# NSA stage of a 13-stage fp32 kernel: gates computed transposed, values unit one place earlier, position additions between two evictions

## The reference, cut to what matters

```python
q, k_c, v_c, k_s, v_s, k_w, v_w, gates = split(h @ w_in)        # 1024 + 6*256 + 48 columns
gates = sigmoid(gates).reshape(B, S, 3, G, R)                   # 48 per token
def compress(kv, pos, w1, w2):                                  # 15 blocks of 32 tokens
    blk = kv[:, cmp_idx] + pos                                  # position additions
    return gelu(blk @ w1) @ w2                                  # (60, 2048) @ (2048, 256) @ (256, 64)
kc, vc = compress(k_c, ...), compress(v_c, ...)
o_cmp = softmax(q @ kc.T, mask) @ vc
o = gates[0] * o_cmp + gates[1] * o_slc + gates[2] * o_win      # o_slc, o_win: causal attention
return o @ w_out
```

## Time and profile before

| | us |
|---|---|
| median of 3 runs | 2328.58 (2327.27 to 2328.65) |
| the profiled execution | 2329.75 |
| its span | 2327.9 |
| mean granted clock | 0.983 |
| PE, DVE, ACT busy | 2261.5, 1780.5, 1159.4 |

### The profile page before, as it was taken

How to read it: one execution, slowest core, us unless ns; L and a number is a source line. 1 busy time by engine, 2 the same in 40 slices (tenths; PEclk the granted TensorE clock), 3 DMA queues, 4 the chain that set the end, 5 groups by cost and what they waited for, 6 DMA issues and landing times.

```text
span 2327.9 us, 37353 instructions
## 1 busy us (share of the span) xinstructions
PE 2261.5 (97%) x14904; PEld 2012.6 (86%) x14904; DVE 1780.5 (76%) x3490; ACT 1159.4 (50%) x2082; POOL 0.2 (0%) x4
## 2 busy tenths in 40 slices
PE   7999999999999999999999999999999999998998
PEld 7968889898889988897988887788888889978997
DVE  7588987779887798777798865577877876478877
ACT  4486554565553555447655634534222235375333
POOL 0000000000000000000000000000000000000000
PEclk9799999999999999989999999999999999999999
DMA  6315666446565565641565532023554522423653
GB/s 239 116 43 206 239 197 215 152 163 233 199 212 186 191 239 192 223 170 38 182 234 198 183 115 85 1 73 120 171 189 154 165 89 100 136 83 133 236 202 118
DMA packets 70155, 373.52 MB, mean 160 GB/s; under 512 B 7392, under 2 KB 16736, under 8 KB 37984
## 3 DMA queue, kind: packets, MB, share of 16 engines
q1 hardware_dynamic: 61472, 361.52, 45.5%
q10 hardware_dynamic: 8512, 9.63, 1.4%
HBM read 369.03 MB, written 1.05 MB: 159 GB/s over the span
## 4 chain that ended last, share of the span: by engine, by line
PE 84%; DVE 9%; ACT 3%; DMA 3%; issue 1%; ACTq 0%; DVEq 0%
PE ps L470 79%; DVE w_lo L1682 3%; DMA w_raw<-weights 2%; PE ps L793 2%; DVE hid_f L2051 1%; PE ps L776 1%; DVE hid_f L2071 1%; ACT w_hi L1128 1%; PE ps L731 1%; PE ps L721 1%; DVE a_both L1682 0%; DVE X L1934 0%; DVE X L1808 0%; ACT p_ring L1260 0%; DMA sm<-small 0%
## 5 line engine op out<-in xcount | busy, mean ns | idle before, releaser
L470 PE MATMUL ps<-a_both,w_hi 128*128 128x256 f32 (+1 forms) x4960 | 1209.4, 330 | 27.6 <-DVE a_both L1739 10.6
L470 PEld LDWEIGHTS ps<-a_both,w_hi 128*128 128x128 f32 x4960 | 828.7, 192 | 105.3 <-issue 29.0
L470 PE MATMUL ps<-a_both,w_lo 128*128 128x256 f32 (+1 forms) x3184 | 902.1, 292 | 0.0
L1682 DVE TENSOR_TENSOR w_lo<-w_raw,w_hi 128x1024 fp32r<-128x1024 f32 (+1 forms) x632 | 707.9, 1148 | 88.4 <-ACT w_hi L1128 81.8
L470 PEld LDWEIGHTS ps<-a_both,w_lo 128*128 128x128 f32 x3184 | 608.2, 191 | 26.3
L1128 ACT CAST w_hi<-w_raw 128x1024 fp32r<-128x1024 f32 (+2 forms) x452 | 418.5, 975 | 417.1 <-DMA w_raw<-weights 416.3
L470 PE MATMUL ps<-hid_both,w_hi 128*128 128x512 f32 (+1 forms) x2088 | 578.3, 355 | 8.4 <-DVE hid_both L1682 5.6
L470 PEld LDWEIGHTS ps<-hid_both,w_hi 128*128 128x128 f32 x2088 | 367.1, 190 | 65.8 <-DVE hid_both L1682 4.4
L470 PE MATMUL ps<-hid_both,w_lo 128*128 128x256 f32 (+1 forms) x1396 | 421.1, 305 | 0.0
L470 PEld LDWEIGHTS ps<-hid_both,w_lo 128*128 128x128 f32 x1396 | 265.2, 190 | 14.4
L1134 ACT CAST w_hi<-w_raw 128x1024 fp32r<-128x1024 f32 (+2 forms) x180 | 183.6, 1020 | 0.6 <-DMA w_raw<-weights 0.6
(11 more groups left out here) (215 smaller groups left out, 1957.1 us busy)
## 6 DMA issues: line engine op xcount, KB each, us to landing
w_raw<-weights SPq DMA_DIRECT2D x250, 1024.0 KB, 4.8
pe_sb<-weights SPq DMA_DIRECT2D x96, 512.0 KB, 5.6
w_raw<-weights SPq DMA_DIRECT2D x64, 704.0 KB, 4.0
pe_sb<-na_bias ACTq DMA_DIRECT2D x32, 128.0 KB, 2.2
X<-x_t SPq DMA_DIRECT2D x2, 512.0 KB, 7.1
X<-c_rows ACTq DMA_DIRECT2D x2, 512.0 KB, 4.1
qk<-qk ACTq DMA_DIRECT2D x4, 256.0 KB, 7.0
qk<-ctx_t ACTq DMA_DIRECT2D x1, 1024.0 KB, 5.7
```

Of the source, the lines that this page charges most:

```text
L470: return nc.tensor.matmul(out, stationary, moving, start=start, stop=stop)
L1682: return v.tensor_tensor(out, a, b.bitcast(F32), ALU.subtract)
```

## The change

It does three things. (1) The gates are made transposed: the 48 gate columns of the weights are stationary, the 256 tokens moving, 24 matmuls in place of 48. ScalarE copies the 48x256 result from PSUM to `t_ring`, TensorE transposes it back in two pieces into bank 5, and ScalarE's sigmoid reads that and signals `gates`, for which TensorE waits ahead of turn 1's scores. The gelu transposes now stand ahead of the gates. (2) The stage's units have another order: 0, 1; queries 2 to 4; 5 compress(0,0); 6 query; 7 compress(0,1); 8 keys; 9 compress(1,0); 10 keys; 11 compress(1,1); 12 values; 13 small; the rest as it was. (3) VectorE makes the position additions between the two evictions of units 1 to 4, and the `w_lo` work of unit 14 stands behind the gelu copies.

On TensorE:

```diff
-                for _ in range(4):
+                for _ in range(3):
                     fm_unit("AA", a)
...
-                compress(0, 0)
-                fm_unit("AA", a)
-                compress(0, 1)
-                fm_unit("AA", a)
-                compress(1, 0)
+                for kv in range(2):
+                    for h in range(2):
+                        compress(kv, h)
+                        if (kv, h) != (1, 1):
+                            fm_unit("AA", a)
                 values_unit()
-                compress(1, 1)
-                u, [(gb, gp, (g_ready, _)), (kb, kp, (k_ready, _)), (vb, vp, (v_ready, _))] = start_unit("AAD")
-                start_product("A", gp)
-                for tt in range(2):
-                    c0 = 2 * P + 2 * HD
-                    last = tm(ps[:, gb, tt * 3 * HEADS:(tt + 1) * 3 * HEADS], u % SLOTS,
-                              lambda k: slice(c0 + k * 3 * HEADS, c0 + (k + 1) * 3 * HEADS),
-                              raw_tokens(tt))
-                last.then_inc(g_ready, 1)
                 pe.wait_ge(nsa[j]["gelu"], 2)
...
                 last.then_inc(nsa[j]["gelu_t"], 1)
+                u, [(gb, gp, (g_ready, _)), (kb, kp, (k_ready, _)), (vb, vp, (v_ready, _))] = start_unit("AAD")
+                start_product("A", gp)
+                c0 = 2 * P + 2 * HD
+                for k, (xh, xl) in enumerate(a):
+                    c = slice(c0 + k * 3 * HEADS, c0 + (k + 1) * 3 * HEADS)
+                    weights_at(c)
+                    out = ps[0:3 * HEADS, gb, 0:S]
+                    mm(out, w_hi[:, u % SLOTS, c], xh, k == 0, False)
+                    mm(out, w_hi[:, u % SLOTS, c], xl, False, False)
+                    last = mm(out, w_lo[:, u % SLOTS, c], xh, False, k == KD - 1)
+                last.then_inc(g_ready, 1)
                 pe.wait_ge(nsa[j]["gelu_ready"], 2)
...
                 last.then_inc(v_ready, 1)
+                pe.wait_ge(nsa[j]["gates_copied"], 1)
+                for tt in range(2):
+                    last = nc.tensor.transpose(ps[:, GATE_BANK, tt * 3 * HEADS:(tt + 1) * 3 * HEADS], gates_t[:, tt * P:(tt + 1) * P],
+                                               ident[0:3 * HEADS, 0:3 * HEADS])
+                last.then_inc(nsa[j]["gates_t"], 1)
...
                         pe.wait_ge(nsa[j]["cmp_shifted"], 1)
+                        pe.wait_ge(nsa[j]["gates"], 1)
```

On ScalarE:

```diff
-                for tt in range(2):
-                    ins = nc.scalar.activation(gate[:, tt, :], ps[:, bank, tt * 3 * HEADS:(tt + 1) * 3 * HEADS], ACT.Sigmoid,
-                                               scale=stat[:, tt:tt + 1])
-                ins.then_inc(taken["A"], 1)
+                nc.scalar.copy(gates_t, ps[0:3 * HEADS, bank, 0:S]).then_inc(s["gates_copied"], 1)
...
-                ins.then_inc(taken["A"], 1)
+                ins.then_inc(taken["A"], 2)
+                act.wait_ge(s["gates_t"], 1)
+                for tt in range(2):
+                    ins = nc.scalar.activation(gate[:, tt, :], ps[:, GATE_BANK, tt * 3 * HEADS:(tt + 1) * 3 * HEADS], ACT.Sigmoid,
+                                               scale=stat[:, tt:tt + 1])
+                ins.then_inc(s["gates"], 1)
                 ahead(u)
```

On VectorE:

```diff
+                def unit_around(dst, between):
+                    u, made = next_unit("AA")
+                    scaled(made[0], dst(0))
+                    between(u)
+                    scaled(made[1], dst(1))
+                    ahead(u)
...
+                ahead(scaled_unit(compressed(0)))
                 sync()
-                dve.wait_ge(taken["A"], cnt.n["A"])
-                add_positions(0, False)
-                query(1)
-                dve.wait_ge(s["shifted"], 32)
-                add_positions(0, True)
-                query(2)
+                unit_around(compressed(1), lambda u: first_positions(0))
+                unit_around(queries(0), lambda u: first_positions(1))
+                unit_around(queries(1), lambda u: moved_positions(0))
                 blocks_low(0)
-                add_positions(1, False)
-                query(3)
-                add_positions(1, True)
+                unit_around(queries(2), lambda u: moved_positions(1))
+                skip("")
+                ahead(scaled_unit(queries(3)))
                 step(v.memset(vg_hi.bitcast(F32), 0.0))
                 skip("")
+                blocks_low(1)
                 ahead(keys(0))
-                blocks_low(1)
...
-                values("DD", 0, KV)
-                skip("")
+                values_unit, made = next_unit("DD")
+                evict_values(range(2), made, 0, KV)
...
                 ins.then_inc(s["gelu_ready"], 1)
+                ahead(values_unit)
                 ahead(u)
```

More of the change, by code:

```diff
@@ L223, in program @@
                for n in ("nsa0", "nsa1", "moba0", "mla0", "na0")}
-        nsa = [{e: sem(f"{e}{j}") for e in ("shifted", "blocks", "blocks_hi", "blocks_ready", "gelu", "gelu_t", "gelu_ready", "cmp_scores",
+        nsa = [{e: sem(f"{e}{j}") for e in ("shifted", "blocks", "blocks_hi", "blocks_ready", "gelu", "gelu_t", "gelu_ready", "gates_copied",
+                                            "gates_t", "gates", "cmp_scores",
                                             "cmp_shifted", "cmp_exp", "cmp_p", "cmp_t", "cmp_t_taken")}
@@ L398, in program @@
         GEL_BANK = 4
+        GATE_BANK = 5
+        gates_t = t_ring[0:3 * HEADS, 0, 0:S]
         c_act = [X[:, KD // 2 * j:KD // 2 * (j + 1), CTX] for j in range(2)]
@@ L1390, in run_nsa @@
                 skip("")
+                skip("AA")
+                u, _ = next_unit("")
+                gelu(1, u)
+                ahead(u)
                 skip("DD")
-                skip("")
-                gelu(1, cnt.n["unit"] - 1)
                 u, made = next_unit("AAD")
@@ L2142, in run_nsa @@
                 norm_row()
-                for kv in range(2):
-                    ahead(scaled_unit(lambda pair: k_sb[:, 4 + kv, pair * S:(pair + 1) * S]))
                 v_rep = [h.rearrange("p (m g r c) -> p m g r c", m=2, g=GROUPS, r=REP) for h in (vg_hi, vg_lo)]
@@ L2165, in add_positions @@
                     ins.then_inc(s["blocks"], 1)
-                def query(i):
-                    ahead(scaled_unit(lambda m: q_sb[:, 2 * i + m, 0:S]))
                 def keys(br):
@@ L2176, in blocks_low, with compressed, first_positions, moved_positions @@
                     minus(blk_lo[:, c], blk_f[:, c], blk_hi[:, c]).then_inc(s["blocks_ready"], 1)
-                query(0)
-                sync()
-                dve.wait_ge(taken["A"], cnt.n["A"])
-                add_positions(0, False)
-                query(1)
-                dve.wait_ge(s["shifted"], 32)
-                add_positions(0, True)
-                query(2)
+                def compressed(kv):
+                    return lambda pair: k_sb[:, 4 + kv, pair * S:(pair + 1) * S]
+                def unit_around(dst, between):
[3 more added lines that the diff above has]
+                    scaled(made[1], dst(1))
+                    ahead(u)
+                def first_positions(kv):
+                    dve.wait_ge(taken["A"], 2 * kv + 2 + before)
+                    add_positions(kv, False)
+                def moved_positions(kv):
+                    dve.wait_ge(s["shifted"], 32)
+                    add_positions(kv, True)
+                def queries(i):
+                    return lambda m: q_sb[:, 2 * i + m, 0:S]
+                before = cnt.n["A"]
+                ahead(scaled_unit(compressed(0)))
+                sync()
+                unit_around(compressed(1), lambda u: first_positions(0))
+                unit_around(queries(0), lambda u: first_positions(1))
+                unit_around(queries(1), lambda u: moved_positions(0))
                 blocks_low(0)
-                add_positions(1, False)
-                query(3)
-                add_positions(1, True)
+                unit_around(queries(2), lambda u: moved_positions(1))
+                skip("")
+                ahead(scaled_unit(queries(3)))
                 step(v.memset(vg_hi.bitcast(F32), 0.0))
                 skip("")
+                blocks_low(1)
                 ahead(keys(0))
-                blocks_low(1)
                 step(v.memset(vg_lo.bitcast(F32), 0.0))
```

12 lines of the change are left out of this document (6 added, 6 removed).

## The result

The changed kernel takes 2309.07 us (median of 4 runs, 2307.88 to 2310.39), the kernel before 2328.57 (4 runs, 2327.27 to 2328.65). The ratio is 0.9916, with a 95% interval of 0.9905 to 0.9927: 19.5 us faster. The forecast was 2305.5 in a range of 2299 to 2315. The profiled execution took 2308.13 us. The title has the values unit one place earlier. By the order of the units it stands one place later (12, it was 11), behind the last compress unit.

A forecast was written before the change was run, and what follows sets the result against it. TensorE, busy 2261.5 of 2327.9 us, was taken to bound the kernel. Stage gains of 14.1 and 11.0 us, less 2 for the clock, gave 23.1: 2306.65 profiled, 1.17 above the median, so 2305.5, range 2299 to 2315.

The forecast's parts named there:

- Up to the small unit: Units 1 to 12: eviction wait of 0.86 us gone, waits of 0.9 and 0.3 added, values end at 79.4.
- Gates: Small unit at full clock: 24 gate matmuls in 2.73 us, against 8.1 before; v product ends at 85.9.
- The chain through VectorE: Sigmoid, cast and w_lo of unit 15, value copies, mask, p_cmp: its transposes start at 97.35, TensorE waiting some 3 us.
- The clock term: Short fall to half clock from the v product through the compressed scores: 1 us per stage, between 0 and 3.5.
- the 77.15 us without it: Forecast length of each NSA stage, unit 1 to first p_cmp transpose, before the clock's price; 91.27 and 88.17 before.
- the slack of some 3 us before L902: TensorE's forecast wait for p_cmp before its first transpose, some 3 us, said to take up a late clock fall.
- 1 (no fall): Clock doesn't fall between the v product and turn 1: gain 25.1 us, time 2303.5; chance 0.22.
- 2 (low until turn 1): Clock falls with the v product, down until turn 1: gains 7.6 and 4.5 us, time 2316.5; chance 0.12.
- 3 (low for the turns): Clock falls at waits before p_cmp's transposes, down for 16 turns: costs 44 us in both stages, 2349; chance 0.02.
- 4 (VectorE late): Compress run: VectorE doesn't keep up, units 6 and 9 wait 4 us more per stage, 2313.5; chance 0.09.
- The number: Whole kernel: 23.1 us less, from 2329.75 to 2306.65 for a profiled execution, 2305.5 for the median.
- the likeliest case: Whole kernel, forecast with a short clock fall: 2305.5 us, range 2302 to 2309; chance 0.52.

The follow-up runs named there:

- kernels 6: Changed kernel with blocks_low(1) ahead of unit 9's w_lo work and the w_lo copies of unit 15 moved behind p_cmp; 2306.95 us.
- kernel 7: Changed kernel with the 24 matmuls of v in each NSA stage moving 256 columns where 64 are used; 2307.66 us.
- kernel 8: Changed kernel with the four gelu transposes put back behind the gates' matmuls; 2319.16 us.
- 10: Changed kernel with blocks_low(1) ahead of unit 9's w_lo work and v's matmuls moving 256 columns; 2305.47 us.
- kernel 1: Kernel before with only the gates formed transposed, unit order and position additions as they were; 2325.22 us, ratio 0.9988.
- 2: Changed kernel with the old gate matmuls of 48 moving columns, new unit order kept; 2326.8 us, ratio 0.9994.
- 3: Changed kernel with the position additions back behind both evictions and the w_lo work of the unit two ahead; 2312.7 us.
- kernel 5: Kernel before with its 48 gate matmuls widened from 48 to 256 moving columns, the extra ones unused; 2325.03 us.
- 9: Changed kernel with the old 48 gate matmuls, widened from 48 to 256 moving columns; 2316.23 us.
- 12: Kernel 10 with unit 15's w_lo copies behind p_cmp, ScalarE's table loaded early and compressed-score matmuls moving 128 columns; 2300.32 us.

## Why the prediction was right, step by step

- **Up to the small unit**: right. The wait before unit 4 is gone, compress(1,0) waits 1.12 us (forecast 0.9), unit 6 waits 0.79 (0.3, within its bounds; in kernels 6, 7, 8 and 10 it is 0.28 to 0.42). The values unit ends at 79.6 (79.4).
- **Gates**: right, 82.91 - 80.12 = 2.79 us for 24 (2.73), at full clock, and no wait before them or before the k product. v ends at 86.3 (85.9).
- **The chain through VectorE**: right as to its members and its end, 97.73 us (97.3). That TensorE would wait for it some 3 us was wrong for this kernel: the clock had used up that slack. Kernels 7 and 10, where the clock stayed up, show the wait at 1.16 to 2.31 us.
- **The clock term**: a short fall behind the v product was forecast and came, at 88.5 in the compressed scores. Its price was set at 1 us a stage; against the 77.15 us without it the stages took 77.91 and 79.12, so 0.8 and 2.0. Both stay within the 0 to 3.5 given. The stretches of 6.9 and 10.2 us cost TensorE 3.0 and 4.5 us, and the slack of some 3 us before L902 took up the rest, as the prediction had argued. How long they would be it had not worked out from anything; that they came out as they did is luck. The term also priced the clock apart from the rest, as if the other terms would stand without it. Kernels 1 and 2 refute that: neither part brings its own sum.
- **Rivals.** 1 (no fall) is not what this kernel does; kernel 7 nearly does, and its stages take 77.51 and 77.58 us where the rival has 77.15. Its median is 2307.7 all the same, and not 2303.5. 2 (low until turn 1) is what kernel 8 comes near in its first stage. 3 (low for the turns) didn't occur: the clock is 1.00 from 95.4 to the second stage, and in the changed kernel the moba stage's wait of 2.64 us, at 438.2, has no fall behind it either. 4 (VectorE late) cost 0.5 us more than forecast at unit 6 and 0.2 at unit 9, not 4. That VectorE's queue has no idle time there was read too strictly: before the change it stands idle 0.85 us at 43.7.
- **The number.** 23.1 us were forecast between profiled executions, 2329.75 - 2308.13 = 21.6 came: 0.7 from the clock term, 0.7 from between and behind the stages. The other 2.1 us of the difference to 2305.5 come from taking the profiled execution to lie 1.17 above the median; this one lay 0.94 below it. The measured 2309.07 lies at the upper end of the 2302 to 2309 that were given for the likeliest case, and all of these differences point the same way.

What stays open: the low stretch differs from execution to execution, and the runs have one profile each, so the price of a single part within a microsecond or two isn't settled. The changed kernel's own execution lacks the stretch of 3.4 or 6.8 us at 1.2 GHz (1.5 or 3.0 us of time) which the kernel before and all numbered kernels but 3 have in the moba stage. Nor was a wait taken out of kernel 1 alone.

## What to carry to other kernels

Where TensorE has a run of matmuls with few moving columns, read the granted clock first: turning the operands so that the many columns move, or moving columns that nobody needs, can be worth more than its own time (3.4 us in kernel 5, 10.6 in 9; in 7 and 12 nothing that the medians tell apart). A wait in the same place cost more than twice its length in kernel 8. Parts that work through the clock must be tried together, since each alone may show nothing. Before shortening a chain on another engine, look whether TensorE waits at its end now; if not, bring the clock up first and then do both.
